# A scratch tensor in DRAM laid out block by block instead of unit by unit

## The reference

```python
h = rmsnorm(x, g_ffn)
q = (h @ w_query).reshape(C, 8, 2, 128)                 # 8 heads, 2 halves
s = einsum('chpd,hpkd->chpk', q, sub_keys)              # scores against 2 x 128 keys
sv, si = top_k(s, 16)                                   # in each half
cand = sv[:, :, 0, :, None] + sv[:, :, 1, None, :]      # 256 sums a head
top_s, pos = top_k(cand.reshape(C, 8, 256), 16)
idx = experts of those (first key * 128 + second key)   # of 16384 experts
gate = softmax(top_s)
hid = gelu(einsum('cd,chkd->chk', h, expert_u[idx])) * gate
x = x + einsum('chk,chkd->cd', hid, expert_v[idx])      # 128 experts a token
y = rmsnorm(x, g_final)
```

## Time and profile before

| what | value |
|---|---|
| median of 3 runs | 2985.82 us |
| profiled execution, its own time | 2985.82 us |
| its span | 2984.0 us |
| mean granted TensorE clock | 0.951 |
| TensorE busy | 2620.7 us (88%) |
| VectorE busy | 2071.2 us (69%) |
| GpSimd busy | 1526.6 us (51%) |
| moved by DMA | 961.55 MB, mean 322 GB/s |

### The profile page before, as it was taken

How to read it: one execution, slowest core, us unless ns; L and a number is a source line. 1 busy time by engine, 2 the same in 40 slices (tenths; PEclk the granted TensorE clock), 3 DMA queues, 4 the chain that set the end, 5 groups by cost and what they waited for, 6 DMA issues and landing times.

```text
span 2984.0 us, 30618 instructions
## 1 busy us (share of the span) xinstructions
PE 2620.7 (88%) x9973; PEld 1499.7 (50%) x9973; DVE 2071.2 (69%) x4568; ACT 481.9 (16%) x910; POOL 1526.6 (51%) x1284
## 2 busy tenths in 40 slices
PE   7989868879978889767589899999999999999997
PEld 6785546535634465334255444444444455444543
DVE  1437876686087768456688977977777777777778
ACT  2321601120136014122130000010000000000001
POOL 0002574455455750222525566776666676666675
PEclk9999989989989999889799999999999999999999
DMA  4376897788787984666898999999999999999998
GB/s 155 114 233 216 274 381 289 264 316 293 278 299 254 368 305 132 215 205 208 285 324 335 375 384 410 392 378 396 410 410 411 408 405 410 407 410 409 408 410 317
DMA packets 361185, 961.55 MB, mean 322 GB/s; under 512 B 28000, under 2 KB 152672, under 8 KB 359008
## 3 DMA queue, kind: packets, MB, share of 16 engines
q0 software_dynamic: 184320, 671.17, 59.5%
q1 hardware_dynamic: 126048, 259.52, 23.9%
q10 hardware_dynamic: 50688, 29.36, 3.3%
HBM read 930.58 MB, written 29.36 MB: 322 GB/s over the span
## 4 chain that ended last, share of the span: by engine, by line
PE 31%; DMA 28%; issue 17%; DVE 16%; POOL 5%; ACT 3%; POOLq 0%; DVEq 0%; ACTq 0%; SPq 0%
PE bank L615 17%; DMA ring<-in_expert_v,idx 15%; DMA ring<-in_expert_u,idx 12%; PE bank L603 6%; POOL ring L1234 5%; DVE ring L1269 5%; PE o_bank L632 3%; DVE region_a L1286 3%; DVE consts L1640 2%; PE bank L668 1%; ACT region_s L1034 1%; DVE neg_max L1358 1%; DVE consts L1634 1%; PE bank L593 1%; DVE region_q L1530 1%
## 5 line engine op out<-in xcount | busy, mean ns | idle before, releaser
L1234 POOL DMA_INDIRECT ring<-in_expert_u,idx x640 | 781.5, 1221 | 753.4 <-DVE idx L1541 315.1
L1234 POOL DMA_INDIRECT ring<-in_expert_v,idx x640 | 744.9, 1164 | 684.0 <-PE o_bank L632 397.1
L1269 DVE CUSTOM_DVE_ANT_0 ring<-ring,h 128x1024 f32<-128x1024 f32 x640 | 766.0, 1224 | 184.0 <-DMA ring<-in_expert_u,idx 177.9
L892 PE MATMUL bank<-wslot,gate_attn 128*128 128x512 f32 x1536 | 705.8, 610 | 70.4 <-DVE gate_attn L1577 66.1
L882 PE MATMUL o_bank<-region_b,wslot 128*128 128x384 f32 x2048 | 681.3, 486 | 1.9 <-DVEq L1610 1.9
L1286 DVE SCALAR_TENSOR_TENSOR region_a<-ring,dots,region_a 128x1024 f32<-128x1024 f32 x384 | 493.1, 1284 | 152.8 <-DMA ring<-in_expert_v,idx 130.0
L882 PEld LDWEIGHTS o_bank<-region_b,wslot 128*128 128x128 f32 x2048 | 389.0, 190 | 300.8 <-issue 63.1
L892 PEld LDWEIGHTS bank<-wslot,gate_attn 128*128 128x128 f32 x1536 | 295.9, 195 | 438.7 <-issue 327.0
L1141 ACT ACTIVATE gate_attn<-o_bank 128x384 f32<-128x384 f32 x128 | 62.7, 490 | 1287.7 <-PE o_bank L882 1254.4
L632 PE MATMUL o_bank<-ring,gate_attn 128*32 128x512 f32 x1024 | 146.5, 698 | 112.5 <-DMA ring<-in_expert_v,idx 105.2
L615 PE MATMUL bank<-region_b,wslot 128*128 128x128 f32 (+2 forms) x768 | 231.7, 459 | 2.8 <-ACT region_b L928 2.8
(11 more groups left out here) (171 smaller groups left out, 1901.6 us busy)
## 6 DMA issues: line engine op xcount, KB each, us to landing
wslot<-in_expert_uT SPq DMA_DIRECT2D x128, 512.0 KB
wslot<-in_expert_v SPq DMA_DIRECT2D x128, 512.0 KB
wslot<-in_w_in SPq DMA_DIRECT2D x34, 1024.0 KB
wslot<-in_w_query SPq DMA_DIRECT2D x24, 1024.0 KB
expert_weights<-region_p ACTq DMA_DIRECT2D x24, 1024.0 KB
wslot<-in_w_out SPq DMA_DIRECT2D x12, 1024.0 KB
region_s<-expert_weights SPq DMA_DIRECT2D x8, 1536.0 KB
region_p<-expert_weights SPq DMA_DIRECT2D x8, 1536.0 KB
```

The lines of the kernel that those rows point to most:

```text
L892: ins = nc.tensor.matmul(dense_out[2 * t + n][:], hidden[q][:, t * P:(t + 1) * P], v_cols[slot][:, n * 512:(n + 1) * 512], start=start, st ...
L1234: nc.gpsimd.indirect_dma_start(ring[:, n % RING, :], None, expert_u if what == "u" else expert_v, bass.IndirectOffsetOnAxis(ap=ids, axis=0 ...
L1269: nc.vector.tensor_tensor_reduce(row, row, h2[:, H2_AT[k], :], 1.0, 0.0, ALU.mult, ALU.add, dots[:, DOTS_AT[k] + s:DOTS_AT[k] + s + 1]).th ...
```

## The change

The scratch tensor gets another order of its dimensions. Before it was (partition, unit, block, 8 columns x 16 tokens); now it is (partition, block, column, token).

- A store writes, on each partition, 8 KB. Before, these went to 16 places of 512 bytes each, one in each unit. Now they are one run of 8 KB.
- A load reads, on each partition, 12 KB. Before, they were one run of 12 KB. Now they are 24 pieces of 512 bytes, one in each block.

The number of DMAs, the engines and queues that issue them, their order, their waits, their bytes, and what lies where in the on-chip buffers are as before. No instruction of any engine moves.

```diff
-        weight_dram = nc.dram_tensor("expert_weights", (P, UNITS, BLOCKS, UNIT_COLS * BLOCK), F32, kind="Internal").ap()
+        weight_dram = nc.dram_tensor("expert_weights", (P, BLOCKS, N_KEYS, BLOCK), F32, kind="Internal").ap()
...
-                sp.dma_start(weights_in[u % PLACES].rearrange("p (b n) -> p b n", b=BLOCKS),
-                             weight_dram[:, u, :, :]).then_inc(weights_loaded[u % PLACES], 16)
+                sp.dma_start(weights_in[u % PLACES].rearrange("p (b j t) -> p b j t", j=UNIT_COLS, t=BLOCK),
+                             weight_dram[:, :, u * UNIT_COLS:(u + 1) * UNIT_COLS, :]).then_inc(
+                                 weights_loaded[u % PLACES], 16)
...
-                    act.dma_start(weight_dram[:, :, block, :],
-                                  blocks[block % 2].rearrange("p (u n) -> p u n", u=UNITS)).then_inc(
-                                      block_stored[block % 2], 16)
+                    act.dma_start(weight_dram[:, block, :, :].rearrange("i j t -> i (j t)"),
+                                  blocks[block % 2]).then_inc(block_stored[block % 2], 16)
```

## The result

The changed kernel took 3024.78 us (median of 4 runs, 3020.02 to 3028.17), the kernel before 2986.05 us (2985.24 to 2987.16). The ratio is 1.0129, with a 95% interval of 1.0111 to 1.0146: 38.7 us slower, where 12.5 us were forecast. The time lies within the stated range of 2976 to 3032, but the loss is three times the forecast one. The profiled execution took 3016.60 us with a span of 3014.8 us, 30.8 us more than the profiled one before; it was faster than all four of these runs, so its trace shows the effect somewhat too small.

The account below looks back on a forecast made before the run. The DMA engines were taken to bound the dense stage. 2985.8 us, plus 21.5 for its loads, minus 9 in the storing stage, gave 2998.3 us; own range 2990 to 3010 (56%), 8-in-10 range 2976 to 3032.

Parts of the forecast that it names:

- The bound: Dense stage: DMA engines are tighter than TensorE; one microsecond more DMA work a unit costs about one, from about 1800 us.
- Packet counts: Whole kernel: after the change q10 has about 4600 packets and q1 about 173000.
- The price of a small read: Weight loads: a 512-byte packet takes 28.2 ns, a load 5.4 us of every engine instead of 3.8, +1.65 us a load.
- The storing side: Storing stage: each store 1.1 us shorter, little of it on the path; -9 us together, ends 0 and -14.
- The five waits beside a store: Storing stage, loop over c: waits for gathered rows with a store in flight shrink; -6 us.
- The wait of 13.39 us at the end: End of the storing stage: this store's wait goes, copies end about 2 us sooner, last store lands 1.1 us sooner; -3.
- The first load: Start of the dense stage, 1548 us: two loads go out, the first lands some 1.65 us later; +1.7.
- The loads issued before 1820 us: Dense stage, the next two loads, DMA share below 1: the engines' idle tenth hides 1.65 us each; cost nothing.
- the drawn-out load: Dense stage: a weight load taken in turns with gathers lasts 20 to 25 us; the total doesn't change.
- Turns between the queues: Dense stage: gathers get nearly everything during a load; u piece in time or just about, TensorE's wait moves some 15 us.
- Rival 1: Dense stage: load over 30 us, u piece some 10 us late, TensorE stands, then engines idle; +54, about 3031 us; 14%.
- The turns: DMA engines: with two queues working, packets are taken in turn singly, whatever their size; by the skill's rule the total stays.

Follow-up runs that it names:

- The two moves on the kernel before: Kernel before, each load cut into four of 6 blocks ahead of four columns: ratio 1.0002; kernel before, 14 dense-stage loads issued by ScalarE on q10: 0.9997.
- four portions: Changed kernel, each load cut into four of 6 blocks, issued ahead of four columns in succession: 2998.76 against 2989.99 us, ratio 1.0036.
- own queue: Changed kernel, the 14 dense-stage weight loads issued by ScalarE on q10 instead of SyncE: 2999.93 against 2985.97 us, ratio 1.0050.
- stores alone: Changed kernel with 8 KB stores, but each load reading one 12 KB run a partition (wrong weights): 2984.07 against 2989.99 us, ratio 0.9980.
- the place behind the u piece: Changed kernel, whole load issued just behind its column's u piece instead of just ahead: 3001.44 against 2986.74 us, ratio 1.0046.
- the three moves: Changed kernel with loads in four portions (ratio 1.0036), on ScalarE's queue q10 (1.0050), or just behind the u piece (1.0046).
- the loads in 1 KB: Kernel before, scratch with a 512-byte gap after every second block, so loads come in 1 KB packets: 2998.49 against 2989.99 us, ratio 1.0030.

## Why the prediction was right and wrong

- **The bound: right.** The DMA share stayed at 1.0 and more, and load work that the change added came out as time. The two moves on the kernel before, which change no packet time to speak of, changed nothing.
- **Packet counts: right**, to the packet (4608 and 173152).
- **The price of a small read, 28.2 ns: right as a size.** It was forecast as +19.8 us in twelve units and +21.5 in all. With nothing late behind them, the same packets cost 17 us (four portions) and 21 us (own queue) by the runs, 18.9 and 21.1 us in the dense stages of these profiles. In the middle of the gathers, too, a 512-byte packet took 27 ns in the median (2108 to 2120 us), as in the last store. At the start of the stage two loads in a row show it, in the changed kernel; the last store had 290 GB/s:

```profile
1542.00:1550.00 8.00, 8.00 (x27) 4.69 (x26) 6.78 (x58) 0.49 (x1) 0.00 (x0) 1.00 1.02 285
```

  The Trainium skill's rule that transfers run at line rate from 512 bytes on ("DMA: Bandwidth & Descriptors", section "Specifications") is not what this chip did for reads either: 285 against 418 GB/s.
- **The storing side: right in place, perhaps somewhat too high.** -9 us were forecast; it was -7.8 between the two traces, -8.2 between the means of all profiles, -6 by the runs (-1.5 to -10 by the interval). The chain of the changed kernel, against the earlier trace rows:

```profile
1200.20 5.87 DMA ring<-in_expert_v,idx
...
1407.92 12.55 DMA ring<-in_expert_v,idx
...
1536.56 3.85 DMA expert_weights<-region_p
...
1540.48 9.13 DMA region_s<-expert_weights
```

  The five waits beside a store fell from 40.88 to 36.02 us in sum, 4.9 where 6 were credited; the last of them did not shrink (11.24 before, 12.55 after), so a shorter store did not take its excess away. The wait of 13.39 us at the end is gone. The first load landed 3.1 us later (9.13 for 6.04), not 1.65.
- **The loads issued before 1820 us: taken at nothing, and that was too little.** The two in question, of 1632.1 and 1725.7 us, were followed by waits for u pieces of 8.17 and 11.94 us. From the first weight load to the one at about 1821 us it took 272.2 us before and takes 281.7. How much of the 9.5 is scatter is open: stores alone took 276.6 for it.
- **The step that failed: the drawn-out load.** Under "Turns between the queues" the prediction put the load at 20 to 25 us, the u piece behind it "in time or just about", and said that this "moves TensorE's wait by some 15 us and doesn't change the total, as long as some queue always has work". Two things in it were wrong. The length: I let the gathers leave 2.4 us of every column to the load. In fact they took their turn nearly always (1116 packets against 1176), a load lasted 35 and 40 us in the two cases shown, and the u piece came up to 12.5 us after TensorE wanted it. And the condition: queues don't always have work. When TensorE waits for a u piece, VectorE's fixed order stops the gathers, the ring fills, and once the piece is there the prefetch is full. In the second case shown that left 10 us at 213 GB/s, and over the stage the gaps grew by 14 us. Four portions, an own queue, and the place behind the u piece each took most of this share away with the packets as they are. By the runs it is 38.7 + 6 - 17 = 28 us with four portions as the measure of the packets' own time, and 24 us with the own queue. The term was priced at 0. Why the runs give 24 to 28 us and the gaps of the trace only 14 is in part that the profiled execution was a fast one and that the gaps are counted from 1820 to 2900 us alone; the rest stays open.
- **Rival 1 was the case**, with a chance of 14% and 3031 us. Its mechanism (u piece late, then idle engines) is shown by the waits, by the gaps and by the three moves; its condition, a load of over 30 us, was met. That its 3031 us lie so near the 3024.78 is in part luck: it put the dense stage at +54 us, the packets' own time included, where it was +38.6.
- **The turns.** The prediction held that an engine takes single pieces in turn, against the Trainium skill's packets of 9 to 17 descriptors ("DMA: Bandwidth & Descriptors", section "Queues, rings and completion order"). Its reason was not sound: if gathers and small pieces both went nine to a turn, the load would be drawn out just the same, and equal counts would come out as well. The starts of the packets in the trace decide it. Between 2108 and 2120 us two small packets start 180 to 190 ns apart twice as often (2220 pairs) as at the distances around it, and 20 to 30 ns apart no more often than elsewhere (1218 pairs). 188 ns are one gathered piece of 160 ns and one small one of 28; small pieces in a row would start some 28 ns apart. So the trace agrees with single pieces and not with nine to a turn.

## What to carry to other kernels

A layout of a scratch tensor decides which of two stages gets the small packets; give them to the one in which the DMA engines have room. Here they cost 0.2% in the storing stage and 1.46% in the dense one. Beside their own time, small packets make a transfer long wherever another queue has large ones, since the queues here took turns by packets and not by bytes. Before small packets go into a queue, look at what is queued behind them and when it is needed; portions, or a queue of their own, cost nothing on the kernel before (1.0002 and 0.9997) and took back 0.93 and 0.79 of the 1.29% on the changed one.

## What the runs showed of the hardware

- SyncE could not issue further while many of the small packets were pending: the issue behind such a load took 23.05 us instead of 0.43, and the v piece after it 0.96 to 3.67. That the queue takes only a limited number of packets is my reading of it; no run here shows the number. What this adds to the u piece's lateness was not tried by itself: the own queue takes away both the stopped issues and the place behind the load.
- A queue of small packets gets few bytes beside one of large packets: 0.60 MB against 4.06 in 12 us, at nearly equal counts of packets. With the load on a third queue beside gathers and columns, one of 1.5 MB took some 48 us.
- The kernel before spread over 2 us beside the changed one, and over 12 to 17 us in the later rounds; the changed one's four runs spread over 8. So the spread tells nothing of late pieces.
- The small packets' own time goes about with their number: 10.3 us in the last column of the table for the loads in 1 KB, 20.3 for those of 512 bytes in four portions, 2.9 for the kernel before. The extra packets an engine and load are 88 and 184.
